# Moving one modulation third from VectorE to TensorE, and a mixer's loads, in a two-block kernel

## The reference, cut to what matters

```python
mod = silu(c) @ ada_w[layer] + ada_b[layer]          # 1024 -> 6 * 1024
sh1, sc1, g1, sh2, sc2, g2 = jnp.split(mod, 6, axis=-1)
h = rmsnorm(x, norm_mix[layer]) * (1.0 + sc1) + sh1
x = x + g1 * mixer(h)
h = rmsnorm(x, norm_ffn[layer]) * (1.0 + sc2) + sh2
x = x + g2 * ffn(h)
```

## Time and profile before

| | us |
|---|---|
| median of 3 runs (lowest, highest) | 2362.14 (2361.83, 2362.47) |
| profiled execution, its time | 2359.98 |
| its span, first to last instruction | 2358.2 |
| PE busy, share | 1893.3, 80% |
| DVE busy, share | 1350.3, 57% |
| ACT busy, share | 327.7, 14% |
| mean DMA rate | 379 GB/s |
| granted TensorE clock, mean | 0.945 |

### The profile page before, as it was taken

One profiled execution on the slowest core, in us unless ns is written; L12 is line 12 of the kernel. 1 busy time (PEld: TensorE's weight loads), 2 busy tenths in 40 slices (PEclk: granted clock), 3 DMA queues, 4 the chain that ended last, 5 costly groups with the idle time before them and its releaser, 6 DMA issues. The chain is left out here.

```text
span 2358.2 us, 24683 instructions
## 1 busy us (share of the span) xinstructions
PE 1893.3 (80%) x9175; PEld 1016.0 (43%) x9175; DVE 1350.3 (57%) x3272; ACT 327.7 (14%) x822; POOL 560.6 (24%) x568
## 2 busy tenths in 40 slices
PE   6998767666678799898877777799989988777776
PEld 4665433333366464444423222275645433222222
DVE  3633000000057758768877876657677688778766
ACT  1052000000021430110000000123310100000001
POOL 1000000000000114444434343200144444344332
PEclk9999888778889899999999999999999999999999
DMA  9987999999989349999999999897499999999997
GB/s 388 411 258 314 431 428 430 427 431 428 414 292 393 110 189 395 422 421 421 394 421 421 421 421 421 352 362 267 192 417 421 422 421 415 421 412 420 410 421 322
DMA packets 147191, 894.78 MB, mean 379 GB/s; under 512 B 18460, under 2 KB 30588, under 8 KB 63868
## 3 DMA queue, kind: packets, MB, share of 16 engines
q0 software_dynamic: 73728, 536.90, 55.0%
q1 hardware_dynamic: 73340, 356.25, 37.9%
HBM read 889.68 MB, written 3.42 MB: 379 GB/s over the span
## 5 line engine op out<-in xcount | busy, mean ns | idle before, releaser
L1954 PE MATMUL psum<-sb_area 128*128 128x512 f32 x2048 | 975.5, 613 | 242.3 <-DVE sb_area L2666 238.9
L2692 DVE CUSTOM_DVE_ANT_0 sb_area<-sb_area 128x1024 f32<-128x1024 f32 x512 | 626.1, 1224 | 280.8 <-DMA sb_area<-in_peer_uv,sb_peer_e 278.7
L804 POOL DMA_INDIRECT sb_area<-in_peer_uv,sb_peer_e x512 | 542.9, 1060 | 999.9 <-PE psum L1954 731.3
L1954 PEld LDWEIGHTS psum<-sb_area 128*128 128x128 f32 x2048 | 373.5, 193 | 725.1 <-DVE sb_area L2666 380.7
L1608 PE MATMUL psum<-sb_area 128*32 128x256 f32 x2048 | 175.1, 517 | 127.7 <-DMA sb_area<-in_moe_w_gu 125.2
L2237 DVE COPY sb_area<-psum 128x128 f32<-128x128 f32 x32 | 9.3, 292 | 391.8 <-PE psum L1620 391.8
L1198 ACT ACTIVATE sb_small<-sb_small 128x2 f32<-128x2 f32 x258 | 52.5, 203 | 1148.7 <-DVE sb_small L2692 1148.7
L2666 DVE SCALAR_TENSOR_TENSOR sb_area<-sb_ident,sb_small,sb_area 128x128 f32<-128x128 f32 x512 | 156.6, 346 | 51.2 <-ACT sb_small L1198 46.0
L1608 PEld LDWEIGHTS psum<-sb_area 128*32 128x32 f32 x2048 | 83.9, 147 | 218.3 <-DMA sb_area<-in_moe_w_gu 139.7
L784 POOL TENSOR_SCALAR_AFFINE_SELECT sb_area<-sb_area 128x256 f32<-128x256 f32 x1 | 0.4, 407 | 746.8 <-DVE sb_area L2496 746.8
L1315 PE MATMUL psum<-sb_area 128*128 128x256 f32 x784 | 174.3, 384 | 3.4 <-DVE sb_area L2071 3.2
(11 more groups left out here) (352 smaller groups left out, 1368.5 us busy)
## 6 DMA issues: line engine op xcount, KB each, us to landing
sb_area<-in_moe_w_gu SPq DMA_DIRECT2D x30, 4096.0 KB, 33.4
sb_area<-in_ada_w SPq DMA_DIRECT2D x72, 1024.0 KB, 12.9
sb_area<-in_moe_w_dn SPq DMA_DIRECT2D x32, 2048.0 KB, 24.0
sb_area<-in_peer_w_q SPq DMA_DIRECT2D x8, 2048.0 KB, 13.2
sb_area<-in_sb_w_in SPq DMA_DIRECT2D x6, 2048.0 KB, 21.6
sb_area<-in_odd_w_in SPq DMA_DIRECT2D x6, 2048.0 KB, 11.3
sb_area<-in_even_w_in SPq DMA_DIRECT2D x5, 2048.0 KB, 12.6
sb_area<-in_moe_w_gu SPq DMA_DIRECT2D x4, 2048.0 KB, 20.7
```

The costliest lines, as they stand in the source:

```text
L804: pool.indirect_dma_start(uv_rows[s], None, rows, bass.IndirectOffsetOnAxis(ap=peer_e[:, m:m + 1], axis=0)).then_inc(named(f"uv_loaded{s}" ...
L1954: last = pe.matmul(ps[:, 4 + 2 * t + half, :], diag[:, s, :], uv_rows[s][:, D + half * HALF:D + (half + 1) * HALF], start=(k == 0), stop=( ...
L2692: dve.tensor_tensor_reduce(uv_rows[s][:, 0:D], uv_rows[s][:, 0:D], h_tok[:, m // P, :], 1.0, 0.0, ALU.mult, ALU.add, dots[:, m % BODY:m % ...
```

## The change

The seventh third (n = 48 to 55) goes to TensorE: `SPREAD = (0, 6)` names the thirds that `spread_piece` sums, and `spread_by` and `summed_by` count for the two ways. In rounds 2 to 5 of the even softmax TensorE does two spread pieces each, behind the weighing. `copy_row(6)` moves to round 6 of the softmax on VectorE, behind `normed(5)`; `turn_row(6)` to round 7 on TensorE, ahead of the squared differences, which also wait for `mod_made` of 7; `take_third(6)` to round 7 on VectorE, behind `scored(7)`. `sum_third(6)` goes. VectorE's remaining 16 pieces are spread otherwise (5 and 6 ahead of the index heads, 4 at h = 1, 1 at h = 3), and `take_third(4)` is at h = 3 instead of 5. SP loads 5, 4, 5 and 2 pieces behind groups even[2] to [5], 4 behind even[8] and 4 behind even[9], the first output projection's weights. SP's block of the even mixer waits for the third count of `x_parts` instead of `x_done`.

```diff
--- before.py
+++ after.py
@@ -170,6 +170,16 @@
         def ada_stage(n):
 
             return next((stage, n - first) for stage, (first, last) in BY_STAGE.items() if first <= n < last)
+
+        SPREAD = (0, 6)
+
+        def spread_by(n):
+
+            return KC * SPREAD.index(n // KC) + n % KC + 1
+
+        def summed_by(n):
+
+            return n + 1 - KC * sum(third < n // KC for third in SPREAD)
 
         def ada_turns(n):
 
@@ -570,10 +580,10 @@
                 stage, i = ada_stage(n)
                 ring = ada_ring[stage]
                 used = n - len(ring)
-                if i >= len(ring) and used < KC:
-                    sp.wait_ge(ada_direct, used + 1)
+                if i >= len(ring) and used // KC in SPREAD:
+                    sp.wait_ge(ada_direct, spread_by(used))
                 elif i >= len(ring):
-                    sp.wait_ge(ada_used, used - KC + 1)
+                    sp.wait_ge(ada_used, summed_by(used))
                 third = n // KC
                 k = n % KC
                 w = ADA[third // 3][0]
@@ -691,7 +701,7 @@
             overflow(sp, load_overflow)
             for n, g in groups_of("even")[:2]:
                 load_group(n, g)
-            sp.wait_ge(x_done, x_updates("even"))
+            sp.wait_ge(x_parts, 2 * x_updates("fin1") - 1)
 
             sp.dma_start(lam_vec.rearrange("p a d -> p (a d)"), I["b_lambda_2"].rearrange("e a d -> e (a d)").broadcast_to([P, 4 * HEAD])
                          ).then_inc(named("even_vec_loaded"), 16)
@@ -704,7 +714,7 @@
                          ).then_inc(named("rel_loaded"), 16)
             sp.dma_start(rel_maps[:, :, 0:P], bass.AP(rows, 2 * P - 1, [[MAPW - 1, P], [P * MAPW, REL_HEADS], [1, P]])
                          ).then_inc(named("rel_loaded"), 16)
-            load_mixer("even", BY_STAGE["even"][0], [0, 0, 3, 5, 6, 4, 4, 2, 0, 0, 0], begun=2)
+            load_mixer("even", BY_STAGE["even"][0], [0, 0, 5, 4, 5, 2, 0, 0, 4, 4, 0], begun=2)
             def peer(stage):
                 L = layer_of(stage)
                 for i, (n, g) in enumerate(groups_of(stage)):
@@ -1108,7 +1118,7 @@
             for n, g in even[7:9]:
                 take(n, g)
             take_row("even", 2)
-            act.wait_ge(ada_sums, 7)
+            act.wait_ge(ada_sums, 6)
             softmax_attention("even")
 
             def peer(stage):
@@ -1456,20 +1466,27 @@
 
             def spread_piece(n):
 
-                pe.wait_ge(ada_loaded[n % len(ada_ring["mix1"])], 16 * ada_turns(n))
+                stage, i = ada_stage(n)
+                third, k = n // KC, n % KC
+                ring = ada_ring[stage]
+                slot = i % len(ring)
+                at = ADA[third // 3][1] + k
+                pe.wait_ge(ada_loaded[slot], 16 * ada_turns(n))
+                if k == 0 and third:
+                    pe.wait_ge(mod_made, third)
                 for g in range(4):
-                    last = pe.matmul(ps[32 * g:32 * (g + 1), 7, :], c_silu[:, n:n + 1].broadcast_to([P, 32]),
-                                     ada_ring["mix1"][n % len(ada_ring["mix1"])][:, g * HALF:(g + 1) * HALF],
-                                     start=(n == 0), stop=(n == KC - 1), skip_group_check=True)
+                    last = pe.matmul(ps[32 * g:32 * (g + 1), 7, :], c_silu[:, at:at + 1].broadcast_to([P, 32]),
+                                     ring[slot][:, g * HALF:(g + 1) * HALF],
+                                     start=(k == 0), stop=(k == KC - 1), skip_group_check=True)
                 last.then_inc(ada_direct, 1)
-                if n == KC - 1:
-                    pe.wait_ge(ada_direct, KC)
+                if k == KC - 1:
+                    pe.wait_ge(ada_direct, spread_by(n))
                     pe.sem_inc(ada_rows, 1)
 
             def sum_third(n):
 
                 stage, _ = ada_stage(n * KC)
-                pe.wait_ge(ada_used, KC * n)
+                pe.wait_ge(ada_used, summed_by(KC * n + KC - 1))
                 pe.wait_ge(mod_made, n)
                 for g in range(4):
                     last = pe.matmul(ps[32 * g:32 * (g + 1), 7, :], ones[:, 0:32], ada_acc[stage][n % 2][:, g * HALF:(g + 1) * HALF],
@@ -1755,7 +1772,9 @@
                     if stage == "even" and i == 3:
                         pe.wait_ge(row_loaded, 16 * ROW_TURN["even"])
                     if stage == "even" and i == PAIRS_OF - 1:
+                        turn_row(6)
                         pe.wait_ge(named("diff_act"), 1)
+                        pe.wait_ge(mod_made, 7)
                         for h in range(DIFF_HEADS):
                             last = pe.matmul(ps[32 * h:32 * (h + 1), 7, 0:T], ones[:, 0:32], diff_sq[:, h, :], start=True, stop=True,
                                              skip_group_check=True)
@@ -1773,6 +1792,9 @@
                         project_first("even", (0,))
                     if i >= 3:
                         weigh(i - 3)
+                    if stage == "even" and 2 <= i < 2 + KC // 2:
+                        spread_piece(6 * KC + 2 * (i - 2))
+                        spread_piece(6 * KC + 2 * (i - 2) + 1)
                     if stage == "even" and i == PAIRS_OF + 1:
                         project_first("even", (5, 6))
                     if stage == "even" and i == PAIRS_OF + 2:
@@ -1811,11 +1833,9 @@
                     turn_row(4 + i // 2)
             pe.wait_ge(named("latent_dve"), CKV_TURNED)
             project(*even[7])
-            sum_third(6)
             project(*even[8])
             pe.wait_ge(proj_out, even[8][0])
             make_row("even", 2)
-            turn_row(6)
             pe.wait_ge(proj_out, even[8][0] + 1)
             pe.wait_ge(named("idx_relu_done"), IDX_HEADS)
             softmax_attention("even")
@@ -2150,7 +2170,7 @@
                         dve.tensor_scalar(acc, ring[slot], c, None, ALU.mult).then_inc(ada_used, 1)
                     else:
                         dve.scalar_tensor_tensor(acc, ring[slot], c, acc, ALU.mult, ALU.add).then_inc(ada_used, 1)
-                    dve.wait_ge(ada_used, n - KC + 1)
+                    dve.wait_ge(ada_used, summed_by(n))
 
             def copy_row(n):
 
@@ -2449,8 +2469,12 @@
                 for i in range(PAIRS_OF + 1):
                     if i < PAIRS_OF:
                         scored(i)
+                    if stage == "even" and i == PAIRS_OF - 1:
+                        take_third(6)
                     if i >= 1:
                         normed(i - 1)
+                    if stage == "even" and i == PAIRS_OF - 2:
+                        copy_row(6)
                     if stage == "even" and i == PAIRS_OF:
                         dve.wait_ge(named("diff_pe"), 2)
                         diff_o = oT[:, 4:8, :].rearrange("p h t -> p (h t)")
@@ -2466,7 +2490,7 @@
             step(dve.tensor_tensor(lam_prod[:, :, :], lam_pairs[:, :, 0, :], lam_pairs[:, :, 1, :], ALU.mult))
             dve.tensor_reduce(lam_sum, lam_prod[:, :, :], AX_X, ALU.add).then_inc(named("latent_dve"), 1)
             dve.tensor_scalar(subln_col, subln_raw, 1.0 - LAM_INIT, None, ALU.mult).then_inc(named("latent_dve"), 1)
-            ada_pieces(at, at + 3)
+            ada_pieces(at, at + 5)
             dve.wait_ge(named("latent_act"), 2)
             dve.tensor_scalar(kv_std, kv_ssq, 1.0 / LATENT, EPS, ALU.mult, ALU.add).then_inc(named("latent_dve"), 1)
             dve.wait_ge(named("latent_act"), 3)
@@ -2475,7 +2499,7 @@
                 last = dve.tensor_scalar(ckv_tok[:, t, :], ckv_tok[:, t, :], kv_std[:, t:t + 1], None, ALU.mult)
             last.then_inc(named("latent_dve"), 1)
 
-            ada_pieces(at + 3, at + 11)
+            ada_pieces(at + 5, at + 11)
             dve.wait_ge(named("latent_act"), 4)
             step(dve.tensor_tensor(neg_lam, lam_exp[:, 1:2], lam_exp[:, 0:1], ALU.subtract))
             step(dve.tensor_scalar(neg_lam, neg_lam, -LAM_INIT, None, ALU.add))
@@ -2499,9 +2523,9 @@
                 dve.wait_ge(named("idx_summed"), h + 1)
                 if h in (1, 7):
                     copy_row(4 + h // 7)
-                if h == 5:
+                if h == 3:
                     take_third(4)
-                now = {1: 4, 3: 4, 5: 5}.get(h, 0)
+                now = {1: 4, 3: 1}.get(h, 0)
                 ada_pieces(done, done + now)
                 done += now
 
@@ -2514,8 +2538,6 @@
                     step(dve.match_replace(both_tiles(idx_score, t), idx_top, both_tiles(idx_score, t), TAKEN))
             dve.tensor_scalar(idx_mask, idx_score, TAKEN, NEG, ALU.not_equal, ALU.mult).then_inc(named("idx_masked"), 1)
             dve.wait_ge(named("rel_loaded"), 32)
-            copy_row(6)
-            take_third(6)
             softmax_attention("even", lambda p: rel_maps[:, DSA_HEADS // 2 + p, :].unsqueeze(1).broadcast_to([P, 2, MAPW])
                               if is_diff("even", p) else rel_maps[:, 2 * p:2 * p + 2, :])
```

## The result

| | before | changed |
|---|---|---|
| median, us | 2361.83 (2360.72 to 2362.47, 5 runs) | 2349.44 (2347.65 to 2350.41, 5 runs) |
| ratio, 95% interval | | 0.9944 (0.9933 to 0.9955) |
| profiled execution, us | 2359.98, span 2358.2 | 2349.44, span 2347.7 |

The kernel is 12.4 us faster by the medians. The sum said 9.5, and the profiled executions differ by 10.5. All runs of both kernels in this study together (119 of before, 20 of the changed) have the medians 2361.65 and 2349.2, so again 12.4 us is what has to be explained. The 119 lie between 2358.6 and 2365.7 us.

The account below looks back on a forecast made before the run. TensorE was taken as the chain, with VectorE a second one as long, in the even mixer before the softmax. -12.2 + 2.7 = -9.5 us gave profiled 2350.5, median 2352.6; range 2349.8 to 2358.0.

Parts of the forecast that it names:

- The stall of 8.04 us: TensorE's wait before the sixth third's sum in the even mixer, for VectorE's take_third(4); predicted to go whole.
- the second chain: VectorE's pieces, top-64 search and mask before the softmax; predicted to end at 770.9, with 2 us to spare.
- rivals A to D: Pieces hidden (chance 0.12), softmax at half clock (0.13), another wait replacing the stall (0.08), late pieces making it slower (0.04).
- A: Softmax: the added pieces fit into TensorE's gaps at no cost; -12.2 us, median 2350.0, chance 0.12.
- the walk: Step-by-step timing of loads, VectorE and TensorE from the even mixer's loads through its softmax, giving -12.2 and +2.7 us.
- -12.2 us up to the first scores: Even mixer before the softmax: stall 8.04, fuller clock 2.1, sum_third(6) 1.0 and turn_row(6) 1.05 us saved.
- +2.7 us in the softmax: Even softmax: cost of the seventh third's pieces on TensorE and copy_row(6); bounds nothing and 7.9 us.
- they arrive 1 to 3 us ahead: Softmax: the last four pieces, requested late, land in 4.9 us at the least, before TensorE needs them.
- rival D: Softmax: pieces of rounds 4 and 5 land late; TensorE stands 5.4 us at median landing; slower kernel, chance 0.04.
- 0 behind the softmax: After the softmax no fixed appointment follows, so its shift passes unchanged to the kernel's end.
- On the path that is worth nothing: SP's even mixer loads start 6.8 us earlier; no gain, since TensorE waits for normed rows, only cover for pieces.
- The tie of the two chains: Before the softmax, TensorE's make_row and VectorE's mask end within 0.1 us; mending only one gains nothing.

Follow-up runs that it names:

- experiment 3: Changed kernel with SP's block waiting for x_done again instead of the third x_parts: 2350.56 us, ratio 0.9950.
- experiment 5: w_out[1] and first peer_w_q group held until the seventh third is summed: changed kernel 2348.83 us; with pieces ahead of the turning 2348.22 us.
- a_again2: One of five profiles of the unedited changed kernel; 34.15 us from first scores to squared differences, no wait for the eighth piece.
- experiment 1: Both kernels run again unedited, five profiles each: mean span 2359.84 us before, 2347.12 us changed.
- experiment 2: Kernel before with early loads alone: 2358.63 us; before with take_third(4) at h = 3: 2362.79; changed kernel with it back at h = 5: 2351.01.

## Why the prediction was right in direction and wrong in size

**The direction and the chain were right.** The stall of 8.04 us went whole, the clock came back, `sum_third(6)` and `turn_row(6)` left the chain, the second chain ended 2 us ahead of the first, and the pieces lengthened the softmax. Counted in the one pair of profiles from the experts' end to the residual, the change is 182.69 - 173.20 = 9.5 us, the forecast to a tenth; that is luck in part, since there the first term was 0.6 us better than walked and the second 0.6 worse. None of the rivals A to D is what happened. A's number, 2350.0, is the nearest to the median, but A wanted the pieces for nothing, and they cost 3.4 us. The median moved 12.4 us, to 0.4 us below the range's low end of 2349.8.

**The step that failed** is that the sum ends with the walk: "-12.2 + 2.7", and "a shift at the softmax's end passes to the end of the kernel". Everything that the edit leaves as it is was put at nothing, even[0] as well as the 1540 us behind the softmax. On the means of five profiles these two made 1.4 and 2.0 us; why the second differs stays open. The terms one by one:

- **-12.2 us up to the first scores was -14.2.** With even[0] in its long form it was -12.8 (126.2 to 113.4): 0.6 better than walked. The other 1.4 is even[0]'s short form in three profiles of five, 2.4 us each. I had taken its one recorded length as its length. Whether the change brings the short form about stays open (experiment 3).
- **+2.7 us in the softmax was +3.4.** The walk's delays for pairs 3 to 6 were +1.8, +1.1, +2.0 and +1.6. In the profile, from the first scores on, they are +1.6, +0.8, +1.8 and +2.7: a little too high for three rounds and too low for the last. What was wrong here is "they arrive 1 to 3 us ahead". Piece 55 was issued at 787.2, 15.3 us after the first scores, where the walk had 15.6, but it landed 8.5 us later and not 4.9. The 4.9 us are near the landing of a piece with no other under way, 4.8 to 5.0. Here piece 54 took 6.85 us, and 55, issued 0.86 us behind it, landed 2.5 us after it (experiment 5). The estimate by the Trainium skill (DMA: Bandwidth & Descriptors, Anatomy of one DMA), 4.4 us, is also one for a transfer by itself; the smallest landing here, 4.8 us, is near it, the eighth piece is not. Where the wait was missing (a_again2) the stretch was 34.15 us, that is +2.4, and pair 6 came +1.5 late: without the late piece the walk was right. This is rival D's mechanism at a fifth of its price (1.07 of 5.4 us), and it made the kernel slower than forecast, not faster.
- **0 behind the softmax was -2.0.** Of this, 0.9 lies in the stretch up to the residual, whose length goes by the clock behind the squared differences (experiment 1), and 1.1 behind it. By the ranges this may be spread, by the mean it is more than I allowed. Neither is shown.

**"On the path that is worth nothing"** for the early loads was true of the changed kernel (experiment 3) and not of the kernel before, where VectorE's wait of 5.3 us for a piece lay ahead of the stall's end (experiment 2). The tie of the two chains was right: `take_third(4)` alone gained nothing.

**The range** was built from the change's own unknowns alone, and its low end was the case in which the pieces cost nothing. It had no term for the spread of stretches that the change leaves as they are, though the three runs of before could not show it either: their 0.6 us of spread is far less than the 7 us that 119 runs have. Of the 0.4 us by which the median fell below the range, 0.3 is in the time before itself, 2362.14 by three runs and 2361.83 by five.

**The better version.** The two placements ahead of the turning are the fastest of the complete kernels: 2346.05 for rounds 2 to 5, and 2346.4 and 2346.8 for the gaps of rounds 0 to 3 and 5, against 2349.2 for the changed kernel and 2361.65 for the one before. The profiles' softmax is shorter in the second (30.82 against 31.77), but no difference in time between the two is shown.

## What to carry to other kernels

Two chains that end within 0.1 us of each other have to be shortened together; cut one alone first, to see that it gains nothing, and then take away the work that both share. Where work is added to an in-order engine inside a pipeline, put it ahead of the instruction that the engine waits for, and not ahead of the one that others wait for: the softmax with the same eight pieces, and the copy that came with them, is 3.4 us longer than before with the pieces behind the weighing, and no longer with them ahead of the turning. A landing time read with the queue empty is a lower bound: it is not what a load takes behind others of its own kind. One profile of a kernel with pauses of TensorE is one draw; before a stretch is called untouched, look at it in several.

## What the runs showed of the hardware

The same 32 matmuls after the same pause took 7.39 us in some executions and 9.4 to 10 us in the others, with a granted clock of 0.93 or 0.50 in the same five microseconds. A later stretch that the change doesn't touch took 24.35 us with the clock at 0.62 and then 1.00 in its first two times six microseconds, and 27.30 with 0.50 in both.

Added matmuls shortened a softmax: 30.82 us with eight pieces in its gaps and the clock at 1.00 through the pairs, 32.54 with one piece, the same loads and copies, and 0.60 and 0.91 in the same stretches, 31.4 to 32.1 in the kernel before. The place counts too: ahead of the turnings of rounds 2 to 5 it was 31.77, at nearly the same mean clock over the stretch (0.96 against 0.97).

Of four loads of 1 MB on one queue the first landed after 4.8 to 5.0 us. The fourth, issued 0.86 us behind the third, landed after 6.6 to 8.7 us in five executions of the same kernel, and after 7.5 us in one where nothing was issued behind it for 8.8 us. In all of them it landed 2.5 to 2.6 us after the third, about three times the distance of the two issues.
